# Turned probabilities of two heads in one PSUM bank, copied together, in tile 0 of the attention

## The reference

```python
def causal_block_attention(q, k, v):
    ...
        s = jnp.einsum('bqhd,bkhd->bhqk', qb, k).astype(jnp.float32) * Dk ** -0.5
        s = jnp.where(kpos[None, :] <= qpos[:, None], s, NEG_INF)
        p = jax.nn.softmax(s, axis=-1).astype(v.dtype)
        return jnp.einsum('bhqk,bkhd->bqhd', p, v)
```

## Time and profile before

| | us |
|---|---|
| median of 3 runs | 1002.47 (1001.68 to 1003.77) |
| profiled execution | 1000.74 |
| its span | 999.0 |
| TensorE busy in the span | 978.1 (98%) |
| VectorE busy | 787.6 (79%) |
| ScalarE busy | 492.8 (49%) |

### The profile page before, as it was taken

One profiled execution on the slowest core, in us unless ns is written; L12 is line 12 of the kernel. 1 busy time (PEld: TensorE's weight loads), 2 busy tenths in 40 slices (PEclk: granted clock), 3 DMA queues, 4 the chain that ended last, 5 costly groups with the idle time before them and its releaser, 6 DMA issues.

```text
span 999.0 us, 13630 instructions
## 1 busy us (share of the span) xinstructions
PE 978.1 (98%) x4723; PEld 822.4 (82%) x4723; DVE 787.6 (79%) x1531; ACT 492.8 (49%) x775; POOL 102.8 (10%) x124
## 2 busy tenths in 40 slices
PE   7999999999999999999999999998999999999997
PEld 6888888898888888888888888887879888888886
DVE  4988988756759888887898888866768678988784
ACT  6344453667654534344635344564446564453533
POOL 5000000154511000000200000040001420000000
PEclk9999999999999999999999999999999999999999
DMA  9575756432644576567175564645740433656532
GB/s 313 182 241 182 239 169 207 169 137 86 206 159 161 165 237 203 175 215 250 63 251 191 188 222 156 246 129 177 262 159 2 142 112 127 232 178 221 172 123 85
DMA packets 126639, 178.13 MB, mean 178 GB/s; under 512 B 3162, under 2 KB 103604, under 8 KB 126592
## 3 DMA queue, kind: packets, MB, share of 16 engines
q1 hardware_dynamic: 122544, 170.37, 51.4%
q10 hardware_dynamic: 3232, 5.77, 1.6%
q0 software_dynamic: 816, 1.37, 0.5%
HBM read 176.41 MB, written 1.09 MB: 178 GB/s over the span
## 4 chain that ended last, share of the span: by engine, by line
PE 90%; DVE 5%; ACT 2%; DMA 1%; issue 1%; ACTq 0%; DVEq 0%; POOLq 0%; POOL 0%
PE ps L980 86%; DVE w_lo L1385 2%; PE ps L1017 1%; PE ps L1164 1%; DVE ps L1485 1%; ACT w_hi L700 1%; DMA raw<-in_l_w_in 1%; DMA probt<-in_l_ffn_pre 1%; PE ps L993 0%; PE ps L1210 0%; DVE moba_q L1417 0%; ACT xt_hi L716 0%; ACT down_hi L806 0%; DVE heads L1679 0%; DVE logit L1642 0%
## 5 line engine op out<-in xcount | busy, mean ns | idle before, releaser
L980 PE MATMUL ps<-w_hi,xt_hi 128*128 128x512 f32 (+3 forms) x912 | 354.6, 389 | 1.1 <-DVE w_lo L1385 0.9
L980 PE MATMUL ps<-w_hi,xt_lo 128*128 128x512 f32 (+3 forms) x912 | 351.7, 386 | 0.0
L980 PE MATMUL ps<-w_lo,xt_hi 128*128 128x512 f32 (+3 forms) x912 | 351.6, 386 | 0.0
L1385 DVE TENSOR_TENSOR w_lo<-raw,w_hi 128x2048 fp32r<-128x2048 f32 (+3 forms) x112 | 245.4, 2230 | 49.6 <-ACT w_hi L700 49.5
L700 ACT ACTIVATE w_hi<-raw 128x2048 fp32r<-128x2048 f32 (+3 forms) x118 | 215.1, 1870 | 12.6 <-DMA raw<-in_l_w_in 10.3
L1485 DVE STREAM_TRANSPOSE ps<-h 32x128 f32<-32x128 f32 x640 | 206.5, 323 | 9.4
L980 PEld LDWEIGHTS ps<-w_hi,xt_hi 128*128 128x128 f32 x912 | 171.8, 188 | 34.2 <-DVE w_lo L1385 1.5
L980 PEld LDWEIGHTS ps<-w_hi,xt_lo 128*128 128x128 f32 x912 | 171.6, 188 | 33.6
L980 PEld LDWEIGHTS ps<-w_lo,xt_hi 128*128 128x128 f32 x912 | 171.9, 188 | 32.5
L790 ACT ACTIVATE ht_hi<-ps 128x512 fp32r<-128x512 f32 x40 | 23.9, 598 | 292.9 <-DVE ps L1485 292.9
L980 PE MATMUL ps<-down_hi,ht_hi 128*128 128x512 f32 x320 | 125.0, 391 | 0.4 <-DVE down_lo L1505 0.3
(11 more groups left out here) (193 smaller groups left out, 827.1 us busy)
## 6 DMA issues: line engine op xcount, KB each, us to landing
raw_down<-in_l_ffn_wd SPq DMA_DIRECT2D x44, 1024.0 KB, 5.0
raw<-in_l_ffn_wg SPq DMA_DIRECT2D x42, 1024.0 KB, 7.3
raw<-in_l_ffn_wu SPq DMA_DIRECT2D x42, 1024.0 KB, 9.7
raw<-in_l_w_in SPq DMA_DIRECT2D x5, 2048.0 KB, 8.9
raw<-in_l_w_out SPq DMA_DIRECT2D x4, 2048.0 KB, 7.9
raw<-in_l_w_in SPq DMA_DIRECT2D x2, 1536.0 KB, 8.2
gpost<-in_l_ffn_post ACTq DMA_DIRECT2D x4, 512.0 KB, 5.3
bias<-bias_rows ACTq DMA_DIRECT2D x1, 2048.0 KB, 13.7
```

The source lines that it names most:

```text
L980: return pe.matmul(dst, lhs, rhs, start=start, stop=stop, skip_group_check=True)
L1385: dve.tensor_tensor(part(w_lo), part(raw), part(w_hi).bitcast(F32), ALU.subtract).then_inc(main_lo, 1)
```

## The change

In tile 0, where a head has only 128 keys, heads 2i and 2i + 1 share one bank and one slot of 256 columns: the first at column 0, the second at column 128 (`place`). What is counted in banks and slots is now the copy c, of which a part has 4 for tile 0 and 8 for tile 1 (COPIES = 12). VectorE's copy of an even head in tile 0 is left out; that of the odd head waits for its transpose and copies all 256 columns, and raises pt_copied by 2. Tile 1 still has one copy for each head. TensorE issues the same instructions in the same order as before; its waits are on the copies of the same units' pairs.

```diff
--- before.py
+++ after.py
@@ -263,16 +263,32 @@
         def score_bank(u):
             return ps[:, u % 3, :]
 
-        def turned_bank(u):
-            return ps[:, 3 + u % 3, :]
+
+        COPIES = HEADS // 2 + HEADS
+
+        def copy_of(u):
+            hh = u % HEADS
+            return COPIES * (u // UNITS) + (hh // 2 if u % UNITS < HEADS else HEADS // 2 + hh)
+
+        def last_unit(c):
+            i = c % COPIES
+            return UNITS * (c // COPIES) + (2 * i + 1 if i < HEADS // 2 else HEADS // 2 + i)
+
+        def place(u):
+
+            return P * (u % 2) if u % UNITS < HEADS else 0
+
+        def turned_bank(c):
+
+            return ps[:, 3 + c % 3, :]
 
         def prob_slot(u):
 
             return logit[:, u % 6, :] if u % 6 < 3 else gpost[:, (u % 6 - 3) * SEQ:(u % 6 - 2) * SEQ]
 
-        def probt_slot(u):
-
-            return probt[:, u % 4, :] if u % 4 < 3 else gpost[:, 3 * SEQ:4 * SEQ]
+        def probt_slot(c):
+
+            return probt[:, c % 4, :] if c % 4 < 3 else gpost[:, 3 * SEQ:4 * SEQ]
 
 
         x_landed = [[sem(f"x_landed{t}_{part}") for part in range(2)] for t in range(TILES)]
@@ -1157,12 +1173,13 @@
                 def turn_probs(u):
                     t = u % UNITS // HEADS
                     pe.wait_ge(probs_ready, u + 1)
-                    if u >= 3:
-
-                        pe.wait_ge(pt_copied, u - 2)
+                    c, at = copy_of(u), place(u)
+                    if c >= 3:
+
+                        pe.wait_ge(pt_copied, last_unit(c - 3) + 1)
                     for kt in range(t + 1):
-                        ins = pe.transpose(turned_bank(u)[:, kt * P:(kt + 1) * P], prob_slot(u)[:, kt * P:(kt + 1) * P],
-                                           ident[:, :])
+                        ins = pe.transpose(turned_bank(c)[:, at + kt * P:at + (kt + 1) * P],
+                                           prob_slot(u)[:, kt * P:(kt + 1) * P], ident[:, :])
                     ins.then_inc(pt_ready, 1)
 
                 def values(u):
@@ -1173,7 +1190,8 @@
 
                         pe.wait_ge(head_out, OUT_BEFORE[name] - 1 + t)
                     for kt in range(t + 1):
-                        ins = mm(ps[:, 6 + t, hh * HEAD:(hh + 1) * HEAD], probt_slot(u)[:, kt * P:(kt + 1) * P],
+                        at = place(u) + kt * P
+                        ins = mm(ps[:, 6 + t, hh * HEAD:(hh + 1) * HEAD], probt_slot(copy_of(u))[:, at:at + P],
                                  v_of(kt, hh), kt == 0, kt == t)
                     ins.then_inc(pv_ready, 1)
 
@@ -1566,12 +1584,15 @@
                         dve.tensor_tensor(sink_exp[:, cols], low[:, cols], sinks[:, :], ALU.add).then_inc(sink_added, 1)
 
                 def copy(u):
-                    keys = P * (u % UNITS // HEADS + 1)
+                    c = copy_of(u)
+                    if u != last_unit(c):
+                        return
                     dve.wait_ge(pt_ready, u + 1)
-                    if u >= 4:
-
-                        dve.wait_ge(pv_ready, u - 3)
-                    dve.tensor_copy(probt_slot(u)[:, 0:keys], turned_bank(u)[:, 0:keys]).then_inc(pt_copied, 1)
+                    if c >= 4:
+
+                        dve.wait_ge(pv_ready, last_unit(c - 4) + 1)
+                    dve.tensor_copy(probt_slot(c)[:, 0:SEQ], turned_bank(c)[:, 0:SEQ])\
+                       .then_inc(pt_copied, 2 if u % UNITS < HEADS else 1)
 
                 for n in range(count + LAG_V + 1):
                     if n < count:
```

## The result

| | us |
|---|---|
| before, median of 6 runs beside it | 1002.33 (1001.11 to 1003.77) |
| changed, median of 6 runs | 1007.94 (1005.34 to 1009.28) |
| ratio | 1.0052, interval [1.0035, 1.0069] |
| changed, run again (e1) | 1007.42, ratio 1.006, interval [1.0041, 1.008] |
| profiled execution, before and changed | 1000.74 and 1009.28 (span 999.0 and 1007.2) |

The change makes the kernel slower by 5.6 us, in the second measurement by 5.3; forecast were 5.8 (1008.3 us on the scale of before's 1002.47). The two profiled executions differ by more, 8.5 us. Most of what is over lies where the clock falls in the changed kernel and not in the one before: 0.9 us in swa and 1.8 us in the stretch between mla and slc.

A forecast was written before the change was run, and what follows sets the result against it. TensorE, busy 98% of the span, was taken as the bound. Waits of 1.48 (swa), 1.19 (mla), 1.19 (slc), 0.98 (win) and 0.98 (moba) sum to 5.8 us, on 1002.47 giving 1008.3 us; range 1004.6 to 1011.0.

The forecast's parts named there:

- swa: Part swa, tile 0: like slc with slower logits; first wait 0.56 us, then 0.40, 0.32 and 0.20, sum 1.48 us.
- mla: Part mla, tile 0: same shape at its start as slc, so 1.19 us taken for it, unmeasured row by row.
- slc: Part slc, no tile 1 before it: values(0) waits 0.45 us, the next three 0.34, 0.26 and 0.14; sum 1.19 us.
- a clock below 1.00 in a part of the attention: Sign, anywhere in the attention, that would show the forecast wrong; the clock was at 1.00 through the attention before.
- The wait before values of even units: Tile 0: the copy runs one step later while TensorE's values(u) stays; 0.34 us of waiting per pair in plain steady state.
- The four links: Tile 0, 128 keys: scores load to logits 0.54, to copy 0.21, copy 0.42, to values load 0.06; 1.23 us against 0.89.
- The scaling in VectorE's way: Win and moba starts: output scaling between logits(5) and logits(6) holds VectorE 0.59 us; values(2) of win then 0.58 us late.
- Only the starts cost: Rival, chance 0.13: only the first pair of the three calls and the scaling show; 2.4 us, 1004.9 us.
- It does nothing: Rival, chance 0.08: each paired copy in tile 0 is early enough after all; 1002.5 us.
- faster: Rival, chance 0.04: VectorE was the hidden bound in tile 0 of all parts; gain up to 3.0 us, to 999.5 us.
- VectorE's saved time is worth nothing: Tile 0, 20 pairs: 0.15 us less each, 3.0 us of VectorE, hidden by TensorE's back-to-back work and counted as 0.
- The rival that the clock falls: Rival, chance 0.05: waits thin out TensorE's work in tile 0, clock drops; one fall per part adds 8.8 us, 1017 us.

The follow-up runs named there:

- e2: The changed kernel with LAG_V 6 in place of 5, so TensorE issues values(u) one step later: 1001.67 us, ratio 1.0002.
- e3: The kernel before, own copies and banks, with values of an even tile 0 unit also waiting for the odd unit's copy: 1005.9 us, ratio 1.0036.
- e7: The change in slc, win and moba alone; swa and mla copy head by head as before: 1005.01 us, ratio 1.0034.
- e4: The kernel before with every tile 0 copy taking 256 columns, still one per head: 1002.98 us, ratio 1.001.
- e5: The kernel before with LAG_V 6 in place of 5, values one step later, copies as before: 1001.99 us, ratio 1.0008.
- e6: The changed kernel with VectorE's paired copy issued ahead of the logits of its step in tile 0: 1004.86 us, ratio 1.0027.
- e9: The change in swa and mla alone; the other parts copy head by head as before: 1003.5 us, ratio 1.0018.
- e8: The changed kernel with LAG_T 4 and LAG_V 7, transposes one step later and values two: 1002.05 us, ratio 1.0001.

## Why the prediction was right

The way, the size and the place were right; one thing that it had named as a sign of being wrong came all the same, a clock below 1.00 in a part of the attention (swa), and is taken up at the end. Step by step:

- **The wait before values of even units.** Shown. e2 takes it away and the loss goes; e3 brings it alone and most of the loss comes.
- **The four links.** Load of the scores to logits was 0.54 us forecast and 0.53 measured (768.87 to 769.40); logits to copy 0.21 and 0.34 against 0.21 to 0.22 and 0.35 to 0.36; start of the copy to the load 0.48 against 0.47. In win the delays behind units 2, 4 and 6 were forecast as 0.58, 0.84 and 0.98; VectorE's logits of units 8, 10 and 12 are late by 0.58, 0.83 and 0.96 against the start of the part.
- **The scaling in VectorE's way.** Shown in win: 769.62 to 770.22, and the load at 770.90 is the one of the four that waits longest, 0.45 us.
- **slc** costs 0.15 more than forecast. Logits(8) is followed by its copy 0.52 us later, not 0.35, in the changed kernel:

```profile
757.47 0.42 DVE L1578 CUSTOM_DVE_ANT_0 gpost<-ps,bias 128x256 f32<-128x256 f32 x1 [0.80 <-PE ps L996]
...
757.82 0.08 DVE L1578 DVE_READ_ACCUMULATOR2_ANT low<- 128x1 f32 x1
...
757.99 0.42 DVE L1594 COPY probt<-ps 128x256 f32<-128x256 f32 x1
...
758.47 0.30 PEld L996 LDWEIGHTS ps<-heads,probt 128*128 128x128 f32 x2 [0.51 <-DVE probt L1594]
```

  At 757.82 the logits' last instruction starts; the copy starts 0.17 us after it with its transpose long done. In e7, whose slc has the same order, there is no such hole and slc costs 1.17, the forecast to 0.02. What makes the hole is open.
- **mla** cost 1.14, so slc's start served for mla's. It differs in one thing: before, VectorE reached logits(4) 1.74 us after its first, changed 1.48, as unit 0's copy no longer stands in front. That brought nothing to TensorE, whose logits(6) are 0.35 us late all the same.
- **swa** 1.41 at the high clock against 1.48.
- **TensorE cannot win the time back.** Shown: delays only grow from part to part, and the stretch after moba's last logits is 214.49 us against 214.44.
- **The other rivals.** "Only the starts cost" is out: it gave win and moba 0.47 us each, and they lost 0.97; it gave slc 0.45, and it lost 1.34. "It does nothing" and "faster" are out by the interval of the ratio, which lies above 1 in both measurements.
- **VectorE's saved time is worth nothing.** Shown by e2: 1.0002. Its size was wrong in one place: I said 3 us less busy by the durations of the copies, and it is 1.3. Durations overlap at their ends; by the distance of starts (0.20 for 128 columns, 0.34 for 256) a pair saves 0.06 us, 20 pairs 1.2.
- **What the view of waits shows.** I expected 20 stretches of idle time put down to the copies, 5.8 us in sum. Over the whole span that view has 13 and 4.7 us, in the third call 7 and 2.7 us, where the parts lost 3.3. The short ones are not in it: in win values(0) is 0.11 us late (769.31, where the earlier trace rows moved with the part's start give 763.01 + 6.19) and values(6) 0.14, with no idle time beside their rows above. The measure is the distance of starts.

**The rival that the clock falls** gave the main surprise. The three profiles of the changed kernel have a fall at 233 to 237 us, in swa's tile 0, and a fall of 6.8 us in place of 3.4 before slc, neither of which the profile of before has. But e2, with no waits left, has the one in swa too, and so has e4, whose copies hardly cost anything; e5, with e2's order on TensorE, has not; the granted clock is the figure behind POOL's, first e2, then e5:

```profile
229.70:233.10 3.40, 1.84 (x12) 1.31 (x11) 1.26 (x8) 3.15 (x8) 1.75 (x4) 1.00 0.26 96
233.10:236.50 3.40, 3.40 (x18) 3.40 (x17) 2.23 (x11) 2.50 (x12) 2.85 (x8) 0.50 0.01 2
```

```profile
229.70:233.10 3.40, 1.84 (x12) 1.17 (x11) 1.10 (x7) 2.96 (x6) 1.55 (x4) 1.00 0.32 119
233.10:236.50 3.40, 3.40 (x27) 3.13 (x27) 3.19 (x19) 3.12 (x16) 2.93 (x7) 1.00 0.01 2
```

TensorE was busy 1.84 us in the first stretch of both. And e7, which up to 748 us works as before, has the long fall before slc:

```profile
723.80:730.60 6.80, 6.80 (x19) 5.46 (x20) 0.60 (x4) 0.00 (x0) 0.00 (x0) 0.50 0.92 326
```

e6 and e9 have the waits in swa and no fall (e5 to e8 ran on another chip than e2; e9 ran on e2's). So neither fall needs the waits, and the waits alone do not make them. What the Trainium skill says in "TensorE: Matmul & The Clock Gate", "A second HAM failure mode: psum-queue depth-cycling", of a clock that swings because of short idle times between groups, shows in no part of the third call: not in one of the profiles does the clock fall there, with TensorE waiting for copies up to 0.5 us at a time, in e3 0.6. Over all runs the mean granted clock is 0.9947 for the changed kernel (13 runs) and 0.9951 for before (73), which goes with 0.4 us.

One thing stays open: 5 of the 13 runs of the changed kernel have 0.992, and none of the 73 of before is under 0.994. Nor is one of the 64 runs of e2 and e4 to e8; but e3 has 3 of 11 at 0.993 and e9 1 of 11 at 0.992. So the runs with the lowest clock come only in kernels whose swa has the waits, though not in all of these: e6, with shorter waits in swa, has none in 9. That is hardly chance. What leads from the waits to them is not shown, and the rival is not wholly out. A run at 0.992 is 2.5 us longer than one at 0.997 (1009.0 against 1006.5); the loss in mla, win and moba does not depend on it: it is the same in the profiles of the changed kernel, at 0.992, as in e9's (0.997) for mla and in e7's (0.994) for win and moba.

A fall in swa costs 1.48 us when nothing waits (e2 11.56 less e5 10.07 us from first to last logits, orders alike). On it the waits cost 0.88 to 0.94 (12.43 to 12.49 in the three profiles, less 11.56) and not 1.41. That a slower TensorE gives the copy more of the time it needs would explain it; no run tests that.

## What to carry to other kernels

Merging two small operations saves their engine a little (0.06 us a pair here, by the distance of starts), but the first of the two results now comes with the second: ask what step consumes the first, and whether its engine runs in order with room for the delay. Here the room was one step and the merge used more than that; moving the consumer one step later made the merge free, and still not a gain: the engine that it relieved did not bound the kernel. Work out the room from distances of starts in the timeline, not from durations or busy shares, and look for the odd operation (here the output scaling) that stands in the chain once per stage.

## What the runs showed of the hardware

- The time of one kernel goes with the clock that its execution was granted: runs of before have 999.8 us on the mean at a mean granted clock of 0.997 (21 runs), 1001.8 at 0.995 (20) and 1002.8 at 0.994 (32). Two single profiled executions differed by 8.5 us here, where the medians differed by 5.6; the same parts compared inside the profiles agreed to 0.01 us where the clock did not fall in them.
- The same stretch at the start of swa (229.7 to 233.1 us), with TensorE busy 1.84 of 3.40 us, was followed by a fall in the profile of e2 and by none in that of e5, two kernels with the same order on TensorE, each on its own chip.
- From the end of a VectorE copy to the TensorE weight load that waited for it 0.05 us passed (768.84 + 0.42 = 769.26, load at 769.31), at four of four loads in win.
